# Four-layer latent backbone on one core: softmax normalised before the next row maximum, and the sink as a column of the scores

## The reference

```python
def _sink_attention(q, k, v, sink_logit, scale):
    s = jnp.einsum('bqkgd,bskd->bkgqs', q, k).astype(jnp.float32) * scale
    s0 = jnp.broadcast_to(sink_logit[None, :, :, None, None], s.shape[:-1] + (1,))
    p = jax.nn.softmax(jnp.concatenate([s0, s], axis=-1), axis=-1)[..., 1:].astype(v.dtype)
    return jnp.einsum('bkgqs,bskd->bqkgd', p, v)
```

## Time and profile before

| quantity | value |
|---|---|
| median of three runs | 2455.5 us |
| the profiled execution | 2457.2 us, its span 2455.4 us |
| granted TensorE clock, mean of the span | 0.968 of full speed |
| TensorE matmul busy | 2279.7 us, 93% |
| VectorE busy | 1591.5 us, 65% |
| ScalarE busy | 934.7 us, 38% |
| GpSimd busy | 253.8 us, 10% |
| DMA | 296.59 MB, mean 121 GB/s |

### The profile page before, as it was taken

How to read it: one execution, slowest core, us unless ns; L and a number is a source line. 1 busy time by engine, 2 the same in 40 slices (tenths; PEclk the granted TensorE clock), 3 DMA queues, 4 the chain that set the end, 5 groups by cost and what they waited for, 6 DMA issues and landing times.

```text
span 2455.4 us, 29938 instructions
## 1 busy us (share of the span) xinstructions
PE 2279.7 (93%) x11897; PEld 1847.5 (75%) x11897; DVE 1591.5 (65%) x2845; ACT 934.7 (38%) x1421; POOL 253.8 (10%) x225
## 2 busy tenths in 40 slices
PE   6989899999979989899999988788999999898998
PEld 4867688888866746688888865367888887777997
DVE  2435877777766533877777674667877776855554
ACT  4335443331244321443332144654333222455543
POOL 0000101100010024111110000000110100101111
PEclk8999999999999999999999998999999999898999
DMA  8540434445522210244445521022444454213553
GB/s 288 172 154 4 135 124 136 144 137 175 177 93 85 77 35 29 92 133 142 137 142 177 171 70 60 1 64 74 150 133 137 151 173 153 69 35 121 184 178 120
DMA packets 289906, 296.59 MB, mean 121 GB/s; under 512 B 6419, under 2 KB 288028, under 8 KB 289639
## 3 DMA queue, kind: packets, MB, share of 16 engines
q1 hardware_dynamic: 288125, 290.11, 36.7%
q0 software_dynamic: 1232, 4.42, 0.5%
q10 hardware_dynamic: 409, 0.16, 0.0%
HBM read 293.61 MB, written 1.05 MB: 120 GB/s over the span
## 4 chain that ended last, share of the span: by engine, by line
PE 83%; DVE 11%; DMA 1%; SPq 1%; ACT 1%; issue 1%; POOL 1%; ACTq 0%; DVEq 0%; POOLq 0%
PE lo L573 24%; PE lo L575 23%; PE lo L574 23%; PE modp L527 2%; DVE normed L1276 2%; PE lo L827 1%; PE lo L726 1%; DVE h L1281 1%; PE hi L840 1%; PE lo L747 1%; DVE conv L1273 1%; SPq L479 1%; DVE probs L1428 1%; PE hi L702 1%; DVE probs L1385 1%
## 5 line engine op out<-in xcount | busy, mean ns | idle before, releaser
L573 PE MATMUL lo<-u_hi,w_hi 128*128 128x512 f32 (+1 forms) x2328 | 836.5, 359 | 25.0 <-DVE u_lo L1311 23.9
L574 PE MATMUL lo<-u_lo,w_hi 128*128 128x512 f32 (+1 forms) x2328 | 819.3, 352 | 0.0
L575 PE MATMUL lo<-u_hi,w_lo 128*128 128x512 f32 (+1 forms) x2328 | 819.2, 352 | 0.0
L1227 DVE TENSOR_TENSOR w_lo<-w_raw,w_hi 128x2048 fp32r<-128x2048 f32 (+2 forms) x182 | 406.5, 2234 | 349.0 <-ACT w_hi L928 349.0
L928 ACT ACTIVATE w_hi<-w_raw 128x2048 fp32r<-128x2048 f32 (+2 forms) x182 | 339.6, 1866 | 526.8 <-DMA w_raw<-in_ffn_w_down 257.1
L573 PEld LDWEIGHTS lo<-u_hi,w_hi 128*128 128x128 f32 x2328 | 446.8, 192 | 95.9 <-issue 35.4
L1243 DVE SCALAR_TENSOR_TENSOR mod_acc<-mod_raw,silu_c,mod_acc 128x256 f32<-128x256 f32 x1008 | 496.1, 563 | 0.0
L575 PEld LDWEIGHTS lo<-u_hi,w_lo 128*128 128x128 f32 x2328 | 446.7, 192 | 58.6
L574 PEld LDWEIGHTS lo<-u_lo,w_hi 128*128 128x128 f32 x2328 | 447.3, 192 | 56.2 <-issue 1.2
L573 PE MATMUL lo<-mid_hi,w_hi 128*128 128x512 f32 (+1 forms) x704 | 259.2, 368 | 0.0
L575 PE MATMUL lo<-mid_hi,w_lo 128*128 128x512 f32 (+1 forms) x704 | 255.8, 363 | 0.0
(11 more groups left out here) (242 smaller groups left out, 2166.3 us busy)
## 6 DMA issues: line engine op xcount, KB each, us to landing
w_raw<-in_ffn_w_up SPq DMA_DIRECT2D x88, 1024.0 KB, 5.1
mod_raw<-in_mod_w SPq DMA_DIRECT2D x144, 512.0 KB, 3.7
w_raw<-in_ffn_w_down SPq DMA_DIRECT2D x32, 1024.0 KB, 5.4
mod_unit<-in_mod_w SPq DMA_DIRECT2D x24, 1024.0 KB, 7.0
w_raw<-in_a_w_qkv SPq DMA_DIRECT2D x12, 1024.0 KB, 5.2
w_raw<-in_ffn_w_down SPq DMA_DIRECT2D x16, 768.0 KB, 4.4
w_raw<-in_b_w_in SPq DMA_DIRECT2D x12, 1024.0 KB, 5.1
w_raw<-in_a_w_out SPq DMA_DIRECT2D x8, 1024.0 KB, 5.4
```

The source lines that it names most:

```text
L573: mm(o, h3[:, k, c], x, start=(first and k == 0), stop=False)
L574: mm(o, h3[:, k, c], y, start=False, stop=False)
L575: ins = mm(o, l3[:, k, c], x, start=False, stop=(last and k == nr - 1))
L1227: tt(WL[:, n % 3, 0:words], RAW[:, n % 3, 0:words], WH[:, n % 3, 0:words].bitcast(F32), ALU.subtract).then_inc(lo_ready, 1)
```

## The change

It has four parts.

1. **VectorE's step.** Step x becomes: `normalise(x)` (wait for the exponential, reciprocal, multiply), then `peak(x + 2)` and `negate(x + 2)`. This holds for all three attentions.
2. **The weights of the output projection's second tile.** `hi` and `lo` of that tile leave `attention_in` for the loop of `attention`: on ScalarE behind step 2, on VectorE behind step 3. Again in all three attentions.
3. **The sink in layer 2.** Each row buffer of `probs` is 8 words wider. GpSimd writes the sink logit into the column behind the scores (`sinks`, 48 copies, those from the seventh on each wait for the turn of the half six before; semaphore `sink_set`). The exponential runs over 513 columns and its sum holds the sink; its own exponential and the addition of the sums are gone. ScalarE waits for `sink_set`.
4. **Kind 2 in layer 2.** Its maximum is no longer one reduce of the PSUM bank but two of the operations of kinds 0 and 1 over 256 columns, which scale, add zero columns of the mask and write `probs`; the two exponentials read `probs` instead of PSUM, 257 columns each. The two blocks lie 260 words apart. The negated copy of the sinks at the program's start is gone.

```diff
-            ("probs_t", [P, 4, 3, TOK], 4 * (20 * TOK + ROPE_COLS)), ("probs", [P, 6, TOK], None))
+            ("probs_t", [P, 4, 3, TOK], 4 * (20 * TOK + ROPE_COLS)), ("probs", [P, 6, TOK + 8], None))
...
@@ exps (ScalarE)
                 act.wait_ge(s_max, G + x + 1)
+                if not A:
+                    act.wait_ge(sink_set, x + 1)
...
-                if not A:
-                    nb = 1 if t < 2 else 2
-                    last = f(sl[:, 4, 0:nb], sl[:, 1, 0:nb], ACT.Exp, bias=sinkb[:, 0, h:h + 1])
                 last.then_inc(s_exp, 1)
@@ attention_in (ScalarE)
-                    hi(n0 + t + 2)
-                    if t == 5:
+                    if t < 5:
+                        hi(n0 + t + 2)
+                    else:
                         exps(i, 0)
                         exps(i, 1)
@@ attention (ScalarE)
                         evac(x)
+                    if s == 2:
+                        hi(FIRST["out", i] + 1)
@@ attention_in (VectorE)
-                for t in range(6):
+                for t in range(5):
                     lo(n0 + t + 2)
@@ attention (VectorE)
+                    w = TOK // nb
+                    for b in range(nb):
+                        ins = nc.vector.tensor_tensor_reduce(PB[:, x % 6, b * (CTX + 4):b * (CTX + 4) + w],
+                                                             s_bank(x)[:, b * CTX:b * CTX + w], maskT[:, t % 2, TOK - w:TOK], scale,
+                                                             -3e38, ALU.add, ALU.max, sl[:, 0, b:b + 1])
...
+                def normalise(x):
+                    h, t = HALVES[i][x]
+                    nb = 1 if t < 2 else 2
+                    sl, p = small[:, x % 6, :, :], PB[:, x % 6, :]
+                    dve.wait_ge(s_exp, G + x + 1)
+                    link(nc.vector.reciprocal(sl[:, 3, 0:nb], sl[:, 2, 0:nb]))
+                    for b in range(nb):
+                        c0 = b * (CTX if A else CTX + 4)
+                        s = slice(c0, c0 + TOK // nb)
+                        ins = ts(p[:, s], p[:, s], sl[:, 3, b:b + 1], None, ALU.mult)
+                    ins.then_inc(s_norm, 1)
...
                 def step(x):
-                    ahead_by_2 = x + 2 < NH[i]
...
+                    if x >= 0:
+                        normalise(x)
+                    if x + 2 < NH[i]:
+                        link(peak(x + 2))
+                        negate(x + 2)
...
                         step(x)
+                    if s == 3:
+                        lo(FIRST["out", i] + 1)
@@ sinks (GpSimd, called behind attention_in in layer 2)
+            def sinks(i):
+                G = ahead(NH, i)
+                for x, (h, t) in enumerate(HALVES[i]):
+                    if x >= 6:
+                        pool.wait_ge(p_turned, G + x - 5)
+                    p = PB[:, x % 6, :]
+                    dst = p[:, TOK:TOK + 1] if t < 2 else p[:, CTX:CTX + CTX + 5:CTX + 4]
+                    src = sinkb[:, h:h + 1] if t < 2 else sinkb[:, h:h + 1].broadcast_to([P, 2])
+                    nc.gpsimd.tensor_copy(dst, src).then_inc(sink_set, 1)
```

More of the change, by code:

```diff
@@ L223, in build @@
         q_scale = place("q_scale", [P, 2, 4 * A_HEADS])
-        sinkb = place("sink", [P, 2, C_HEADS])
+        sinkb = place("sink", [P, C_HEADS])
         eps = place("eps", [P, 1])
@@ L724, in turn @@
                             at = kt * (1 if t < 2 else 2) + b
-                            src = kt if t < 2 else 2 * b + kt
-                            last = nc.tensor.transpose(t_bank(i, x)[:, at * P:(at + 1) * P], p[:, src * P:(src + 1) * P],
-                                                       ident)
+                            src = kt * P if t < 2 else (CTX if A else CTX + 4) * b + kt * P
+                            last = nc.tensor.transpose(t_bank(i, x)[:, at * P:(at + 1) * P], p[:, src:src + P], ident)
                     last.then_inc(p_turned, 1)
@@ L1378, in peak @@
                     dve.wait_ge(s_ready, G + x + 1)
[L1379 to L1380 removed]
+                    nb = 1 if t < 2 else 2
                     if A:
[L1382 removed]
+                        return nc.vector.tensor_reduce(sl[:, 0, 0:nb], s_bank(x).rearrange("p (b k) -> p b k", b=nb), AX.X, ALU.max)
                     if x >= 6:
                         dve.wait_ge(p_turned, G + x - 5)
[L1385 to L1386 removed]
+                    w = TOK // nb
[3 more added lines that the diff above has]
+                                                             -3e38, ALU.add, ALU.max, sl[:, 0, b:b + 1])
+                    return ins
                 def negate(x):
@@ L1399, in negate @@
                     ins.then_inc(s_max, 1)
-                def step(x):
-                    ahead_by_2 = x + 2 < NH[i]
-                    if ahead_by_2:
-                        top = peak(x + 2)
-                        top.then_inc(dve_chain, 1)
-                        chained[0] += 1
-                        peaked = chained[0]
-                    if x >= 0:
-                        h, t = HALVES[i][x]
-                        nb = 1 if t < 2 else 2
-                        sl = small[:, x % 6, :, :]
-                        dve.wait_ge(s_exp, G + x + 1)
-                        if not A:
-                            link(tt(sl[:, 2, 0:nb], sl[:, 2, 0:nb], sl[:, 4, 0:nb], ALU.add))
-                        ins = nc.vector.reciprocal(sl[:, 3, 0:nb], sl[:, 2, 0:nb])
-                        ins.then_inc(dve_chain, 1)
-                        chained[0] += 1
-                        inverted = chained[0]
-                    if ahead_by_2:
-                        dve.wait_ge(dve_chain, peaked)
-                        negate(x + 2)
-                    if x >= 0:
-                        dve.wait_ge(dve_chain, inverted)
-                        p = PB[:, x % 6, :]
-                        for b in range(nb):
-                            s = slice(b * CTX, (b + 1) * CTX) if t == 2 else slice(0, TOK)
-                            ins = ts(p[:, s], p[:, s], sl[:, 3, b:b + 1], None, ALU.mult)
-                        ins.then_inc(s_norm, 1)
@@ L1700, in _ @@
                     attention_in(i)
+                    if KIND[i] == 2:
+                        sinks(i)
                 o_squares(2 * i)
```

29 lines of the change are left out of this document (17 added, 12 removed).

## The result

The changed kernel took 2417.72 us, median of 4 runs (2415.65 to 2420.38), against 2455.72 us (2452.63 to 2456.60) of the kernel before in the same comparison. The ratio is 0.9846 with a 95% interval of 0.9831 to 0.9860: faster by 38.0 us. The forecast was 2425 us with 2413 to 2438 around it, so it saw about 30 of the 38 us. The profiled execution of the changed kernel has a span of 2418.5 us, 36.9 less than before.

The account below looks back on a forecast made before the run. Attention was taken as paced by a loop through several engines, none full, with TensorE carrying most of the chain. Savings 24.9 + 2.5 - 1 - 2 + 5.8 + 0 = 30.2 us gave 2425 us, range 2413 to 2438.

Parts of the forecast that it names:

- The ring: Layer 2's loop from scores through maximum, normalisation and turn: 10.6 us a group against 14.32, 24.9 us saved in 19 pairs.
- The three pairs at low clock: Layer 2's pairs before the 19, at granted clock 0.66: TensorE itself taken as the bound, no gain counted.
- the clock comes back sooner: Rival at layer 2's entry: a shorter idle stretch restores full clock, 5 us less, 2420 us; chance 0.07.
- The entry: Start of attention without the weights ahead: 2.5 us saved in layer 2, 4.6 us in layer 0.
- The weights in the loop: Two moved weight operations inside attention, at most 4.2 us: 1 us lost in layer 2, 3 in layer 0.
- nothing in layer 3 on balance: Layer 3's attention: at most 2.3 us to win and 4.2 to lose, taken as 0.
- The prediction's own sign for this: A layer 3 longer by 2 us or more would show the moved weights were priced too low.
- Layer 0: Layer 0's attention: 4.6 us at the entry plus 4.2 in seven waits, less 3 for weights, 5.8 us saved.
- The copies: GpSimd's 48 sink copies in layer 2 get in VectorE's way: 2 us lost, range 4.8 to 35.5.
- The rival in which GpSimd slows the kernel down: Copies in layer 2 each hold VectorE for 1.05 us, 50 us in all, giving 2473 us; chance 0.04.
- The late exponential: Rival in the loop: ScalarE's exponential comes too late, 0.3 us lost in 40 halves, 2437 us; chance 0.07.

Follow-up runs that it names:

- The order alone: Kernel before with only VectorE's new step order in all three attentions, weights at the entry and old sink kept: 2422.40 us, ratio 0.9866.
- the sink alone: Kernel before with only the sink column, GpSimd's copies and kind 2's double maximum; old step order, weights at the entry: 2448.57 us, ratio 0.9970.
- the old ring with the clock mostly held: Kernel before with 44 idle matmuls on TensorE in the idle stretch at layer 2's entry: 2460.16 us, ratio 1.0022.
- another profile of the same code: Changed kernel with the weight operations back at the entry in layer 3 only, same code up to layer 3: 2414.81 us, ratio 0.9827.
- the version without the stall: Changed kernel with the two weight operations behind the end of each attention: 2415.49 us, ratio 0.9828.
- The wide copies: Changed kernel with one more GpSimd copy of 512 columns, to an unused tile, behind each of the 48 sink copies: 2423.17 us, ratio 0.9859.

## Why the prediction was right, and where it was off

**The ring, right.** 10.6 us a group were worked out from single rows and 10.41 measured; the 19 pairs took 68.7 us where 67.1 plus 1 for the weights and 2 for the copies were expected, and 65.75 where neither weights nor a low clock lay in them. The order alone and the sink alone, run by themselves, give the shares: 28.0 us and 5.5 to 7.7 us of layer 2. It was right to count a ring and not busy shares: no engine had been over 70% busy, and the pair could still not go faster. The whole came out within the range also because two misses had opposite signs: 7.7 us not counted in the three pairs, 3.0 us of loss not counted in layer 3.

**The three pairs at low clock: the term that failed.** The prediction said "at half speed TensorE's 3.32 become up to 6.6 for a pair and TensorE itself is the bound, so I count nothing there". They gave 7.7 us. The step failed twice. First, TensorE was not the bound there: a pair took 5.9 us, less than the 6.6, and 4.4 of the 17.66 us were waits for normalisations, so the ring, longer by the slow clock, set the pace there too. That row lay in the trace of before. Second, it took the low clock as fixed for the place, while it changed with the ring. The runs split the 7.7 us: the old ring with the clock mostly held takes 14.32 us, 3.3 less; the new ring at nearly the same mean clock (0.90 to 0.91) takes 11.0 to 11.2, another 3.1 to 3.4; and the last 1.0 or so came because the profile of the changed kernel had the full clock there, which another profile of the same code had not. The prediction had the clock as the rival "the clock comes back sooner", with 0.07 and 5 us; it deserved far more. What decides the clock was not tried beyond these runs.

**The entry, right in size.** Layer 2's first turn came 2.8 us earlier (2.4 in two more runs with the same code there), 2.5 forecast; layer 0's 4.5 us earlier (11.64 behind the first scores, not 16.14), 4.6 forecast.

**The weights in the loop: mis-sized.** 1 us in layer 2, 3 in layer 0 and nothing in layer 3 on balance were taken. On the new order the runs show a loss of 1.8 to 1.9 in layer 2, which cancels the gain of 1.3 to 1.9 at its entry; in layer 0 the version without the stall is 2.4 us shorter; in layer 3 it is 3.8 us. There the prediction bounded the loss by 4.2 and took 0, between it and a possible gain of 2.3. But at this entry nothing waits for the weights: the first turn stands 7.06 to 7.08 us behind the first scores in every run, moved or not. Only the loss was left, and it came almost whole. The prediction's own sign for this, a layer 3 longer by 2 us or more, was seen. The gain of the order in layer 3 was 0.8.

**Layer 0, right**, in sum (5.4 against 5.8) and by terms: the order alone gave 3.9 where 4.2 were forecast, and the moved weights 1.5 on top of it where 4.6 less 3 were.

**The copies: 2 us taken, none found.** They took 0.19 us each, and no normalisation is longer. The rival in which GpSimd slows the kernel down needed 0.77 us a copy. The wide copies show that its mechanism is real but small: 48 copies of 0.61 us, 29 us in all, cost 2.9 us at most. By the rule of the Trainium skill (SBUF — State Buffer, section "Who interferes with whom") whoever starts first holds the shared ports for the whole instruction. The direction agrees with the first pair of rows: the copy was 0.06 us ahead, and the normalisation became longer. The size agrees in part: the copy ended 0.55 us after the start of the normalisation, which became 0.34 us longer. The copy that started with `w_lo` took as long as all of `w_lo`.

**The late exponential, wrong** as a rival: VectorE waited for ScalarE's sums only 0.9 us in all of layer 2.

## What to carry to other kernels

In a loop through several engines, write the ring down as start-to-start times and ask which instruction in it could stand behind the one that releases the next engine; here one change of order brought over 30 us with no work removed. Work that is moved off an entry is not free in the loop: put it where nobody waits behind it, and move it only where something waited for it at the entry. Where a slow clock lies in the stretch that a change makes denser, look first whether the engine waits even there, and do not take the clock as given: price the stretch at both clocks. And before a clock seen in one profile is put down to a change, look at a second profile of the same code.

## What was not expected of the hardware

In the kernel before, TensorE's granted clock fell to 0.5 of full speed during an idle stretch of 4.85 us, and in the old ring, in which TensorE is busy some 70% of the time, it was low for 17 of the 20.5 us from 1506.6 to 1527.1. In the new ring it was low for 3.4 us at the entry of layer 2, in one run for 6.9, in the changed kernel not at all. Runs whose code was the same up to that place had it low at different places of layer 2. Matmuls that nobody reads, 3.15 us of them in a wait of 3.3, kept the clock at 1.00 in a window of 15 us where it had been 0.77. And an fp32 matmul of 128 columns shows as two records and takes 0.23 us, where a transpose of the same size takes 0.11 to 0.12 from start to start (four in the 0.43 us from 1516.54 to 1516.97, eight in the 0.97 us up to 1517.94).
